# A decoder layer with a routed mixture of experts on one core: the router fed with rows before their norm, work moved between queues at four places, and identity transposes put into TensorE's queue

## The chip, the core and the metric

The kernel runs on one core of one Trainium2 chip. The core has five engines, each with a queue of its own that runs in order: TensorE (PE in the profile; its weight loads are PEld), VectorE (DVE), ScalarE (ACT), GpSimd (POOL) and SyncE (SP), which here only issues DMA transfers. Engines wait for each other by semaphores alone. The metric is the time of one execution on the device, in microseconds (us), as the median of several runs; lower is better.

## The reference, cut to what matters

One inference step of a layer for 1024 prompt rows and 8 sample rows of 1024 numbers, all in float32. It has an attention and short-convolution mixer, an output projection with residual, and then this:

```python
tok = concatenate([_rmsnorm(hp, norm_ffn), _rmsnorm(hs, norm_ffn)])       # 1032 rows
lg = tok @ w_rg + b_rg                                                    # 4 groups
p_group = softmax(lg);  g_sel = argmax(lg)
le = (tok @ w_re + b_re).reshape(T, 4, 8)                                 # 8 experts in each group
top_v, top_i = top_k(le[g_sel], 2)
gates = softmax(top_v) * p_group[g_sel]
# for each expert e, on the rows that chose it:
hid = silu(x @ w_gate[e]) * (x @ w_up[e]);  y = hid @ w_down[e]
out = sum over the two experts of gate * y                                # added to the residual
y_prompt, y_sample = _rmsnorm(h, norm_final)
```

`_rmsnorm(x, g)` is `x * rsqrt(mean(x*x) + eps) * g`. So a row's norm is one number for the row (`rsqrt(...)`) times one number for each column (`g`).

## The kernel before, in words

Every product that must be precise is done with a high and a low half: ScalarE rounds a tile to the high half, VectorE subtracts to get the low half, and TensorE does three matmuls (high by high, low by high, high by low). The stages, in order of time:

1. **Projection (to 329 us).** 24 column tiles of `w_in`, 3 groups of 344 rows each. SyncE loads `w_raw` tiles in turn (`load_win`); `amask`, the attention mask, is loaded when all groups are done (line 523).
2. **Prompt attention (to 457 us).** 32 steps: `scores` (line 753), `mask` on VectorE (line 1425, which reads `amask`), exponent on ScalarE, turned probabilities (line 768), values (line 791). TensorE begins `scores(n+1)` when `mask(n)` has taken both its banks.
3. **Output projection and router (to 610 us).** 9 turns p = 0..8 of up to 128 rows. In a turn TensorE does `project(p, half, c)` (lines 832 to 834), VectorE adds the bank to `xres` (`residual`, line 1498), ScalarE squares and takes the root (`root_ffn`, lines 1165 and 1166), VectorE makes the normed rows `h2` (`router_rows`, lines 1506 and 1507), SyncE stores them in DRAM (`store_h2`, line 567), TensorE turns them (`turn_h2`, line 846), ScalarE copies them to `h2T` (line 1175), TensorE multiplies them with the router's 36 columns (`route`, line 856), and VectorE picks group and two experts (`choose_first`, `choose_second`, lines 1523 to 1550). `rank` (lines 866, 869) counts how many rows before this one took the same expert, `slots_of` (lines 1570 to 1578) makes one-hot slots of it, `place` (line 877) sums them into a table of 32 experts by 96 slots. Most of this runs a turn or two behind the projection. After turn 8, `token_rows` (lines 1606 to 1610) makes row numbers of the table and `gidx` (line 1617) gives them to GpSimd (`routed`).
4. **Experts (to 1205 us).** 32 experts, one block of 96 rows each. GpSimd gathers the rows (`fetch`, line 1811), TensorE turns them (`turn_rows`, line 922), then `gate`, `up` (both lines 932 to 934), `turn_hidden` (line 948) and `down` (lines 961 to 963). SyncE loads 6 MB of weights for each expert into two sets of buffers; ScalarE and VectorE split them (lines 1203 and 1712). There is one high tile for each of gate, up and down (`wd_hi` for down), so ScalarE may write the next one only when TensorE is done with the last. `list_further` (lines 1627 to 1640) counts the experts with more than 96 rows; such an expert would get a further block after the 32. `count_tile(8)` (line 1558) brings the last turn into the sum that the matmul on line 906 spreads.
5. **Tail (to 1257 us).** SyncE loads `gfin` and the experts' rows `y`, VectorE adds them (line 1781) and norms the row (line 1794).

## Time and profile before

| | us |
|---|---|
| median of 3 runs (1256.76 to 1258.24) | 1257.4 |
| the profiled execution | 1259.14 |
| its span in the trace | 1257.3 |
| TensorE busy in the span | 1141.1 (91%) |
| VectorE busy | 845.0 (67%) |
| ScalarE busy | 666.0 (53%) |
| mean granted clock of TensorE | 0.959 |

The granted clock is a share of 2.4 GHz; it has two levels here, 1.00 (2.4 GHz) and 0.50 (1.2 GHz). A row of a timeline gives the start in us from the span's start, the duration in us, the engine, the line of the program, the operation, what it writes `<-` what it reads, the shape and how many of them, and in brackets how long the engine had been idle and who released it. The chain of waits is followed back from the last instruction; its shares say where time would have to be saved. A float32 matmul that is not split stands as two rows in the trace (x16 for the 8 of `route`), a transpose as one.

### The profile page before, as it was taken

The numbers are of one execution on the slowest core, as the hardware profiler recorded it, in microseconds if no ns is written. First come the engines' busy times: TensorE is split into PE (matmuls) and PEld (weight loads), VectorE is DVE, ScalarE is ACT, GpSimd is POOL, SyncE is SP. The second block draws the span as 40 slices with busy tenths as digits, with TensorE's granted clock in tenths as the row PEclk, the third lists the DMA queues.
The fourth block names the chain that finished last, engine by engine and source line by source line (L and its number), as shares of the span: only waits on it lengthen the run. The fifth ranks groups of instructions, "written<-read, shape, count | busy, mean of one in ns | idle before, by whom it ended". The sixth has DMA issues, their size and how long they took to land.

```text
span 1257.3 us, 16967 instructions
## 1 busy us (share of the span) xinstructions
PE 1141.1 (91%) x6776; PEld 905.4 (72%) x6776; DVE 845.0 (67%) x1149; ACT 666.0 (53%) x832; POOL 107.5 (9%) x126
## 2 busy tenths in 40 slices
PE   5899999999899989997399999999999999999820
PEld 4899999999677658886267777777777777777510
DVE  6214434331577747776588888888898888888529
ACT  6212231111267753331367777777777777777513
POOL 0003110021000000000111111111111111111000
PEclk9999999999999999998599999999999999999965
DMA  8115435141211042001879999999999999999346
GB/s 252 36 51 170 137 96 197 48 127 59 85 52 41 1 143 90 40 34 66 328 278 388 391 391 393 397 393 390 388 399 388 393 387 389 398 392 387 110 162 267
DMA packets 76256, 287.18 MB, mean 228 GB/s; under 512 B 8240, under 2 KB 32944, under 8 KB 51600
## 3 DMA queue, kind: packets, MB, share of 16 engines
q1 hardware_dynamic: 64496, 250.33, 52.1%
q0 software_dynamic: 11680, 35.75, 8.7%
q8 instruction: 55, 0.90, 0.3%
q14 instruction: 25, 0.20, 0.0%
HBM read 264.87 MB, written 25.32 MB: 231 GB/s over the span
## 4 chain that ended last, share of the span: by engine, by line
PE 88%; DVE 4%; DMA 3%; ACT 3%; issue 1%; SPq 0%; POOLq 0%; ACTq 0%; DVEq 0%
PE psum L934 10%; PE psum L932 10%; PE psum L933 9%; PE psum L677 8%; PE psum L679 7%; PE psum L678 7%; PE psum L961 5%; PE psum L962 5%; PE psum L963 5%; PE psum L832 3%; PE psum L753 3%; PE psum L768 3%; PE psum L834 3%; PE psum L833 3%; PE psum L791 2%; PE psum L922 2%
## 5 line engine op out<-in xcount | busy, mean ns | idle before, releaser
L677 PE MATMUL psum<-h_hi,w_hi 128*128 128x344 f32 x576 | 187.3, 325 | 4.1 <-DVE h_lo L1362 4.1
L679 PE MATMUL psum<-h_hi,w_lo 128*128 128x344 f32 x576 | 185.5, 322 | 0.0
L678 PE MATMUL psum<-h_lo,w_hi 128*128 128x344 f32 x576 | 185.5, 322 | 0.0
L1712 DVE TENSOR_TENSOR w_down_lo<-w_down,w_down_hi 128x2048 fp32r<-128x2048 f32 x64 | 143.8, 2288 | 54.2 <-ACT w_down_hi L1203 54.2
L1712 DVE TENSOR_TENSOR w_gate_lo<-w_gate,w_gate_hi 128x2048 fp32r<-128x2048 f32 x64 | 143.8, 2288 | 20.2 <-ACT w_gate_hi L1203 20.2
L1712 DVE TENSOR_TENSOR w_up_lo<-w_up,w_up_hi 128x2048 fp32r<-128x2048 f32 x64 | 143.8, 2288 | 3.0 <-ACT w_up_hi L1203 0.2
L1203 ACT CAST w_gate_hi<-w_gate 128x2048 fp32r<-128x2048 f32 x64 | 119.3, 1921 | 0.0
L1203 ACT CAST w_up_hi<-w_up 128x2048 fp32r<-128x2048 f32 x64 | 119.2, 1920 | 0.0
L1203 ACT CAST w_down_hi<-w_down 128x2048 fp32r<-128x2048 f32 x64 | 118.7, 1904 | 0.0
L677 PEld LDWEIGHTS psum<-h_hi,w_hi 128*128 128x128 f32 x576 | 109.6, 190 | 6.2 <-DVE h_lo L1362 4.7
L961 PE MATMUL psum<-w_down_hi,hT_hi 128*96 128x512 f32 x256 | 103.3, 403 | 7.8 <-DVE hT_lo L1732 7.8
L678 PEld LDWEIGHTS psum<-h_lo,w_hi 128*128 128x128 f32 x576 | 109.6, 190 | 0.0
L679 PEld LDWEIGHTS psum<-h_hi,w_lo 128*128 128x128 f32 x576 | 109.6, 190 | 0.0
L1310 DVE TENSOR_TENSOR w_lo<-w_raw,w_hi 128x1024 fp32r<-128x1024 f32 x24 | 29.4, 1224 | 111.8 <-ACT w_hi L1040 111.8
L932 PE MATMUL psum<-w_gate_hi,xT_hi 128*96 128x512 f32 x256 | 101.8, 397 | 3.0 <-issue 1.8
L932 PE MATMUL psum<-w_up_hi,xT_hi 128*96 128x512 f32 x256 | 102.3, 400 | 0.0
L934 PE MATMUL psum<-w_gate_hi,xT_lo 128*96 128x512 f32 x256 | 102.0, 398 | 0.0
L933 PE MATMUL psum<-w_gate_lo,xT_hi 128*96 128x512 f32 x256 | 101.5, 397 | 0.0
L962 PE MATMUL psum<-w_down_lo,hT_hi 128*96 128x512 f32 x256 | 101.4, 396 | 0.0
L963 PE MATMUL psum<-w_down_hi,hT_lo 128*96 128x512 f32 x256 | 101.3, 396 | 0.0
L934 PE MATMUL psum<-w_up_hi,xT_lo 128*96 128x512 f32 x256 | 101.1, 395 | 0.0
L933 PE MATMUL psum<-w_up_lo,xT_hi 128*96 128x512 f32 x256 | 100.7, 393 | 0.0
(226 smaller groups left out, 1946.0 us busy)
## 6 DMA issues: line engine op xcount, KB each, us to landing
w_gate<-in_w_gate SPq DMA_DIRECT2D x64, 1024.0 KB, 10.4
w_up<-in_w_up SPq DMA_DIRECT2D x64, 1024.0 KB, 11.3
w_down<-in_w_down SPq DMA_DIRECT2D x64, 1024.0 KB, 11.0
w_raw<-in_w_in SPq DMA_DIRECT2D x24, 512.0 KB, 3.7
y_tile<-y_rows SPq DMA_DIRECT2D x16, 512.0 KB, 6.5
kv<-in_cache_k POOLq DMA_DIRECT2D x24, 256.0 KB, 3.8
kv<-in_cache_v POOLq DMA_DIRECT2D x24, 256.0 KB, 4.5
x_tile<-in_x_prompt SPq DMA_DIRECT2D x8, 512.0 KB, 5.5
```

The source lines that it names most:

```text
L677: mm(ps[:, 0:TC], wh[:, k, :], h_hi[:, k, cols], start=(k == 0), stop=False)
L678: mm(ps[:, 0:TC], wh[:, k, :], h_lo[:, k, cols], start=False, stop=False)
L679: ins = mm(ps[:, 0:TC], wl[:, k, :], h_hi[:, k, cols], start=False, stop=(k == KD - 1))
L753: ins = mm(bank(2 * h, 2)[:, at:at + w], qT[head, m, i * P:(i + 1) * P], kT[head, m, at:at + w], start=True, stop=True)
L932: mm(bank(b)[0:SLOTS, :], xT_hi[:, k, :], hi[:, k, :], start=(k == 0), stop=False)
L933: mm(bank(b)[0:SLOTS, :], xT_hi[:, k, :], lo[:, k, :], start=False, stop=False)
L934: ins = mm(bank(b)[0:SLOTS, :], xT_lo[:, k, :], hi[:, k, :], start=False, stop=(k == KD - 1))
L961: mm(out, hT_hi[:, m, :], wd_hi[:, m, cols], start=(m == 0), stop=False)
L962: mm(out, hT_hi[:, m, :], wd_lo[s][:, m, cols], start=False, stop=False)
L963: ins = mm(out, hT_lo[:, m, :], wd_hi[:, m, cols], start=False, stop=(m == DE // P - 1))
L1203: nc.scalar.copy(dst[:, part, :], src[:, part, :]).then_inc(ready, 1)
L1712: vec.tensor_tensor(dst[:, part, :], src[:, part, :], hi[:, part, :].bitcast(F32), ALU.subtract).then_inc(split, 1)
```

## The change: what it does

- **Start.** The first tiles of x are loaded in another order among `const`, `gmix` and `w_raw`, and ScalarE does one square root on a cell that GpSimd has cleared before it waits for any input.
- **Mask.** `amask` is loaded during the projection, beside `w_raw` (after the sample scores have been turned), into another place.
- **Router.** The transposes take `xres` in place of `h2`, half a row tile at a time (`turn_half`), so they don't wait for the norm. The column factor of the norm is multiplied into the router's weights once (`wr`, `gffn_k`), and the row factor is applied to the 36 results in `choose_first` (two operations in place of two, and a maximum of its own). `h2` is still made and stored, for the gather.
- **Last turn.** The order on VectorE, ScalarE and TensorE is written out anew for turn 8: choosing for turn 7 stands ahead of the last residual, VectorE copies the second half of the last `h2T`, `route(8)` stands right behind `rank(7)`.
- **Transposes of the identity.** 12 stand ahead of `rank(8)` and 16 behind the wait for `routed`; they write bank 0, and nothing reads them.
- **Loads around the routing.** `w_up` of expert 0 goes ahead of the last `h2` store, and `w_up` and `w_down` of expert 1 wait until the first gather has landed. VectorE begins to split the first gate weights when GpSimd has issued that gather (`fetch_issued`).
- **Last expert.** Its high half of `w_down` gets a tile of its own, in the place of the gate's high tile (`wd_hi_end`); `list_further` is moved there. `gfin` is loaded there too, and the two rows of y have a semaphore each.

The core of the diff:

```diff
@@ load_x, amask, loads (SyncE)
             load_x(0)
             sp.dma_start(cst[:], a["const"]).then_inc(const_in, 16)
+            load_x(1)
             sp.dma_start(gmix, a["norm_mix"].partition_broadcast(P)).then_inc(gmix_in, 16)
+            load_x(2)
             load_win(0)
-            load_x(1)
-            load_x(2)
...
+                if t == MASK_AT:
+                    sp.wait_ge(scored, NS + 1)
+                    sp.wait_ge(sT_ready, 1)
+                    sp.dma_start(amask, a["amask"]).then_inc(mask_in, 16)
...
-            sp.wait_ge(group_done, len(groups))
-            sp.dma_start(amask, a["amask"]).then_inc(mask_in, 16)
...
-            for p in range(NT):
+            for p in range(NT - 1):
                 store_h2(p)
             sp.wait_ge(o_ready, 4 * NT)
             load_up(first, 0, 0)
+            store_h2(NT - 1)
+            load_down(first, 0, 0)
             load_gate(first, 1, 1)
-            load_down(first, 0, 0)
+            sp.wait_ge(first.rows_in, 16)
             load_up(first, 1, 1)
             load_down(first, 1, 1)
...
+            sp.wait_ge(first.up_done, NE)
+            sp.dma_start(gfin, a["norm_final"].partition_broadcast(P)).then_inc(gfin_in, 16)
@@ TensorE
-            def turn_h2(p):
-                w = rows(turn[p])
-                pe.wait_ge(h2_ready, p + 1)
+            def turn_half(p, half):
+                t = turn[p]
+                w = rows(t)
+                pe.wait_ge(o_used, 4 * p + 2 * half + 2)
                 if p >= 1:
                     pe.wait_ge(h2T_copied, 2 * p)
                     pe.wait_ge(lg_used, p)
...
+            pe.wait_ge(o_used, 4 * NT)
+            for k in range(12):
+                nc.tensor.transpose(bank(0)[:, (k % 4) * P:(k % 4 + 1) * P], ident, ident)
             rank(NT - 1)
             place(NT - 1)
-            pe.wait_ge(o_used, 4 * NT)
             pe.wait_ge(summed, NT)
             mm(bank(6)[:, NE:2 * NE], ones, r_sum[NT % 2], start=True, stop=True, skip_group_check=True
                ).then_inc(counted, 1)
...
             pe.wait_ge(routed, 1)
+            for k in range(16):
+                nc.tensor.transpose(bank(0)[:, (k % 4) * P:(k % 4 + 1) * P], ident, ident)
             pe.wait_ge(first.rows_in, 16)
             turn_rows(first)
...
-                    down(first, (b - 1) % 2, b - 1)
+                    down(first, (b - 1) % 2, b - 1, wd_hi_end if b == NE else wd_hi)
@@ ScalarE
+            act.wait_ge(table_warm, 1)
+            nc.scalar.activation(stat[0:1, 83:84], stat[0:1, 82:83], ACT.Sqrt)
...
             def upper_down(n):
-                if n >= 1:
+                if n == NE - 1:
+                    act.wait_ge(first.gate_done, NE)
+                elif n >= 1:
                     act.wait_ge(first.y_done, n)
@@ VectorE
+                vec.scalar_tensor_tensor(out=r_g[0:w, t, :], in0=lg[:, 0:NGRP], scalar=scale, in1=rbias[0:w, 0:NGRP],
+                                         op0=ALU.mult, op1=ALU.add)
+                vec.scalar_tensor_tensor(out=r_le[0:w, :], in0=lg[:, NGRP:NR], scalar=scale, in1=rbias[0:w, NGRP:NR],
+                                         op0=ALU.mult, op1=ALU.add).then_inc(lg_used, 1)
+                step(vec.tensor_reduce(gm, r_g[0:w, t, :], X, ALU.max))
...
+            residual(NT - 1, 1, (0,))
+            choose_first(NT - 2)
+            choose_second(NT - 2)
+            residual(NT - 1, 1, (1,))
+            count_tile(NT - 2)
+            dve.wait_ge(h2T_ready, 2 * NT)
+            vec.tensor_copy(h2T[:, 4:8, :], bank(5).rearrange("p (k t) -> p k t", k=4)).then_inc(h2T_last, 1)
+            recip_ffn(NT - 1)
             slots_of(NT - 2)
+            router_rows(NT - 1)
             choose_first(NT - 1)
             choose_second(NT - 1)
             slots_of(NT - 1)
...
+            dve.wait_ge(fetch_issued, 1)
             lower_gate(first, 0, 0)
-            list_further()
+            count_all()
             lower_rows(first, 0)
...
+                if b == NE - 1:
+                    lower_down(first, b % 2, b, wd_hi_end)
                 if b < NE:
                     hidden(first, b)
...
+                if b == NE - 1:
+                    list_further()
...
-                dve.wait_ge(y_in[t % NY], 32 * (t // NY + 1))
...
                 for c in range(2):
+                    dve.wait_ge(y_in[t % NY][c], 16 * (t // NY) + 16)
@@ GpSimd
             fetch(first, gidx[:, 0:1])
+            gp.memset(stat[0:1, 82:83], 0.0).then_inc(fetch_issued, 1)
```

`count_all` is the first part of what `list_further` was: `count_tile(NT - 1)`, a wait for `counted`, and a copy of the counts.

How instructions stand on TensorE at the end of the router stage, before (after the last `project`; `cst` is the identity or a matrix of ones, `h_0` the normed rows of turn 8, `r_both_152` belongs to turn 7 and `r_both_151` to turn 8):

```order
L866 MATMUL psum<-r_both_152,cst 128x32
L869 MATMUL psum<-r_sum_154,cst 128x32
L877 MATMUL psum<-r_first_148,hot_slot_159 96x32
L877 MATMUL psum<-r_second_150,hot_slot_160 96x32
L846 MATMUL psum<-cst,h_0_120 128x128 x8
L856 MATMUL psum<-wr,h2T 128x36 x8
L866 MATMUL psum<-r_both_151,cst 128x32
L869 MATMUL psum<-r_sum_153,cst 128x32
L877 MATMUL psum<-r_first_147,hot_slot_159 96x32
L877 MATMUL psum<-r_second_149,hot_slot_160 96x32
L906 MATMUL psum<-r_sum_154,cst 128x32
L922 MATMUL psum<-cst,x_rows 128x96 x8
```

And with the change, from the same place to `rank(8)`:

```order
L858 MATMUL psum<-cst,xres 128x128 x4
L882 MATMUL psum<-r_both_152,cst 128x32
L885 MATMUL psum<-r_sum_154,cst 128x32
L872 MATMUL psum<-wr,h2T 128x36 x8
L893 MATMUL psum<-r_first_148,hot_slot_159 96x32
L893 MATMUL psum<-r_second_150,hot_slot_160 96x32
L921 MATMUL psum<-cst 128x128 x12
L882 MATMUL psum<-r_both_151,cst 128x32
```

The second half of the turned rows (L858) and `route(8)` (L872) now stand ahead of `place(7)`, and the 12 transposes behind it.

TensorE between `place(8)` and the first expert, with the change and with the semaphores it waits for:

```order
L925 MATMUL psum<-r_sum_154,cst 128x32 [waits summed]
L987 MATMUL psum<-cst 128x128 [waits routed]
L987 MATMUL psum<-cst 128x128 x15
L941 MATMUL psum<-cst,x_rows 128x96 [waits expert_rows_in]
L941 MATMUL psum<-cst,x_rows 128x96 x7
```

The 16 transposes (L987) stand behind the matmul that spreads the counts (L925, before L906), and ahead of the turning of the gathered rows.

VectorE in the same stretch, with the change, from `gidx` on:

```order
L1663 CAST gidx<-r_tab 96x32
L1665 TENSOR_TENSOR r_134<-r_133,r_132 128x9
L1666 TENSOR_TENSOR r_groups<-r_groups,r_131 128x36
L1761 TENSOR_TENSOR w_gate_lo_189<-w_gate_183,w_gate_hi 128x2048 x2
L1592 TENSOR_TENSOR r_sum_154<-r_sum_153,r_both_151 128x32
L1674 COPY r_count<-psum 128x32
L1752 TENSOR_TENSOR xT_lo<-psum,xT_hi 128x384 x2
L1761 TENSOR_TENSOR w_up_lo_191<-w_up_185,w_up_hi 128x2048 x2
```

`r_sum_154`, for which L925 waits, is still written behind the two halves of the gate weights; the operations of `list_further` that stood between it and `xT_lo` are gone from here.

## Rows read from the trace of the kernel before

**Rows 1.** The page, part 4: share of each engine in the chain of waits.
```profile
PE 88%; DVE 4%; DMA 3%; ACT 3%; issue 1%; SPq 0%; POOLq 0%; ACTq 0%; DVEq 0%
```

**Rows 2.** Stretches: us, each engine's busy time, granted clock, DMA share, GB/s.
```profile
176.30:180.90 4.60, 4.60 (x42) 4.31 (x40) 0.00 (x0) 4.44 (x10) 0.00 (x0) 1.00 0.00 0
487.00:588.00 101.00, 100.33 (x560) 85.79 (x559) 75.86 (x245) 27.45 (x58) 0.00 (x0) 1.00 0.09 36
590.00:592.00 2.00, 0.00 (x0) 0.00 (x0) 1.89 (x5) 0.00 (x0) 0.00 (x0) 0.50 0.00 0
594.40:595.70 1.30, 0.51 (x4) 0.51 (x5) 1.11 (x10) 0.00 (x0) 0.00 (x0) 0.50 1.00 309
622.70:630.90 8.20, 6.82 (x21) 4.79 (x22) 6.38 (x10) 2.24 (x3) 0.93 (x1) 0.50 0.19 49
645.00:1184.00 539.00, 539.00 (x2563) 383.40 (x2562) 471.14 (x305) 414.11 (x334) 68.10 (x59) 1.00 0.99 381
1197.40:1200.90 3.50, 3.50 (x9) 2.30 (x10) 0.00 (x0) 0.00 (x0) 0.00 (x0) 0.50 0.00 0
```

**Rows 3.** Timeline at the end of the projection: start, duration, engine, line, operation.
```profile
329.58 1.99 PE L753 MATMUL psum<-kT,qT 64*128 64x512 f32 x8 [0.81 <-DVE cT L1376]
332.13 1.23 DVE L1425 CUSTOM_DVE_ANT_0 scores<-psum,amask 128x1024 f32<-128x1024 f32 x1 [2.80 <-DMA amask<-in_amask]
334.56 3.38 PE L753 MATMUL psum<-kT,qT 64*128 64x512 f32 x8 [2.99 <-DVE stat L1425]
```

**Rows 4.** Timeline of the last router turn.
```profile
582.28 1.87 PE L856 MATMUL psum<-wr,h2T 128*128 128x36 f32 x16
587.44 0.75 DVE L1498 SCALAR_TENSOR_TENSOR xres<-psum,stat,xres 128x512 f32<-128x512 f32 x1 [4.21 <-PE psum L834]
590.60 1.29 DVE L1507 SCALAR_TENSOR_TENSOR h<-xres,stat,gffn 128x1024 f32<-128x1024 f32 x1
595.85 1.95 PE L846 MATMUL psum<-cst,h 128*128 128x128 f32 x8
598.47 3.63 PE L856 MATMUL psum<-wr,h2T 128*128 128x36 f32 x16 [0.68 <-ACT h2T L1175]
602.14 0.19 DVE L1523 TENSOR_TENSOR rl<-psum,rbias 128x32 f32<-128x32 f32 x1 [6.55 <-PE psum L856]
605.52 0.19 DVE L1550 TENSOR_TENSOR r_both<-r_first,r_second 128x32 f32<-128x32 f32 x1
```

**Rows 5.** Timeline from the row numbers to the first expert.
```profile
609.65 0.17 DVE L1617 CAST gidx<-r_tab 96x32 int32<-96x32 f32 x1
609.92 4.48 DVE L1712 TENSOR_TENSOR w_gate_lo<-w_gate,w_gate_hi 128x2048 fp32r<-128x2048 f32 x2
610.71 4.55 POOL L1811 DMA_INDIRECT x_rows<-h_rows,gidx  x1 [316.93 <-DVE gidx L1617]
614.65 0.61 PE L906 MATMUL psum<-r_sum,cst 128*128 128x32 f32 x2 [6.10 <-DVE r_sum L1558]
622.88 1.51 PE L922 MATMUL psum<-cst,x_rows 96*128 96x96 f32 x8 [7.62 <-DMA x_rows<-h_rows,gidx]
625.60 0.71 PE L932 MATMUL psum<-w_gate_hi,xT_hi 128*96 128x512 f32 x1 [1.21 <-ACT xT_hi L1193]
```

**Rows 6.** All gathers of the run: duration ns min/median/max, first and last start.
```profile
L1811 POOL DMA_INDIRECT x_rows<-h_rows,gidx x32: 932/1306/4552, 610.7 to 1149.3; - x32
```

**Rows 7.** The chain of waits at the end, in order of time: start, us, what.
```profile
1190.25 1.91 ACT w_down_hi L1203
1192.17 4.49 DVE w_down_lo L1712 x2
1204.88 1.02 ACT y_rows L1218
1206.67 4.28 DMA y_rows<-y_rows,sidx
1212.95 6.06 DMA y_tile<-y_rows
```

More of the change, by code:

```diff
@@ L259, in program @@
         ot = [pack(f"out_tile{s}", [D]) for s in range(NO)]
-        gfin = pack("gfin", [D])
         fjunk = pack("fjunk", [D])
@@ L383, in program @@
         first = Flow("expert")
-        y_in = [sem(f"y_in{s}") for s in range(NY)]
+        y_in = [[sem(f"y_in{s}_{c}") for c in range(2)] for s in range(NY)]
         gfin_in = sem("gfin_in")
@@ L1172, in copy_h2T @@
                     act.wait_ge(lg_ready, p)
-                for half in range(2):
+                for half in range(halves):
                     act.wait_ge(h2T_ready, 2 * p + half + 1)
@@ L1495, in residual @@
                 x = xres[0:w, t, half * 512:(half + 1) * 512]
-                for c in range(2):
+                for c in branches:
                     dve.wait_ge(o_ready, 4 * p + 2 * half + c + 1)
@@ L1500, in residual, with recip_ffn @@
                     dve.wait_ge(o_used, 4 * p + 2 * half + c + 1)
+            def recip_ffn(p):
+                c, w = p % 2, rows(turn[p])
+                dve.wait_ge(std_f_ready, p + 1)
+                step(vec.reciprocal(rst_f[0:w, c:c + 1], std_f[0:w, c:c + 1]))
             def router_rows(p):
```

130 lines of the change are left out of this document (73 added, 57 removed).

## The prediction

> **What bounds the kernel now.** I read the chain of waits first. TensorE holds 88% of it [rows 1], so the question is where TensorE stands still or runs at half clock. The table of stretches answers that. In the router turns it is busy for 100.3 of 101 us at full clock, and in the experts from 645 to 1184 for all of 539 us [rows 2]. In both the change puts no more work on TensorE and takes none away, and there is no idle time to win. Between these stages lie the holes. The timelines and the end of the chain show four: the wait for the mask at 329 us [rows 3], the last router turn [rows 4], the way from the row numbers to the first expert [rows 5], and the last expert with the tail [rows 7]. The change touches all four. I take its parts in that order, each as time by which everything behind it starts earlier.
>
> **Start.** The tile of x that the chain passes through is the fourth, which has the same bytes ahead of it as before. The early square root saves ScalarE a table load where it waits for data anyway. 0, with 0.5 lost and 1.4 won as ends (1.4 is one transfer of 512 KB at the 381 GB/s of [rows 2]).
>
> **Mask.** Before, VectorE began the first mask at 332.13, released by the load of `amask`. With the mask there it waits for the scores. TensorE began them at 329.58 and was done 1.99 later [rows 3], and VectorE can start some 0.1 to 0.2 behind that, at 331.7. So 0.4 won. The second scores took 3.38 where the first took 1.99, since the clock had halved in 2.99 us of idleness. That idleness shrinks to 2.6. From 587.4 (the last projection ends) TensorE is idle, and at 590.0 it stands at 0.50 [rows 2]: 2.6 us were enough there. So I leave this loss in place; if the clock held, 1.4 more. The load itself moves beside the loads of `w_raw`. A wait is added on SyncE, and queued behind it are the `w_raw` tiles, each loaded two column tiles (some 23 us) ahead of its use; the wait ends with the column tile that is running when it begins. Nothing follows.
>
> **Turns 0 to 7.** The same 8 transposes and the same `route` stand in the queue of TensorE, one wait behind another. The new maximum in `choose_first` is one more small step of VectorE (0.2), which has 25 us to spare in this stretch [rows 2]. The one multiplication of `wr` lies ahead of turn 0, beside the wait for `xres`. 0, between 0.7 won (all that TensorE is idle for) and 0.5 lost.
>
> **Last turn, the largest term.** Before, the last residual ran from 587.44 to 588.19. Then VectorE finished turn 7 and TensorE turned the rows only at 595.85, multiplied them until 602.10 at half clock, and the choice for turn 8 began at 602.14 [rows 4].
> With the change, step by step:
> - `route(7)` ends at 584.15 (582.28 + 1.87). `turn_half(8, 0)` waits until VectorE has taken its logits (0.4) and takes 0.5 (4 transposes; 8 took 1.95 at half clock, so 1.0 at full). The last projection moves back by 0.9 and the last residual ends at 589.1.
> - The second half is turned by 589.7 and copied by VectorE by 590.5 (0.75, as its other pass over 128x512 out of PSUM). Then `route(8)`: 1.87 at full clock gives 592.4; at half clock 3.63 gives 594.1.
> - VectorE meanwhile has the reciprocal (0.2), the slots of turn 7 (1.3, 594.4 to 595.7 [rows 2]) and the normed rows (1.29): it is free at 593.3. TensorE has had no gap above 1 us, so I take 592.4, and VectorE is the later one.
> - The choice took 602.14 to 605.71, 3.6 us, and now 3.8. So turn 8 is chosen at 597.1. The 12 transposes end before that: behind `place(7)` at 592.9, 12 x 0.24 at most gives 595.8. They hide behind VectorE's choice, and cost nothing until the choice ends before them.
> - From there to `gidx` it was 4.1 us (605.71 to 609.82 [rows 4, 5]), and the path is the same.
> So `routed` stands at 601.2 where it stood at 609.8: 8.6 won. With `route` at half clock 7.8; with all of it at full clock 9.2. The store of `h2` for turn 8 goes behind the 2 MB of `w_up` and has from 593.3 to 600 for 0.5 MB; it is hidden by some 3 us.
>
> **From `routed` to the first expert.** Before: 13.1 us from `gidx` to the turning of the rows (622.88), 2.7 more to the first `gate` matmul (625.60). The gather's issue took 4.55 us beside VectorE's split of the gate weights, and 0.93 where it was shortest [rows 5, 6]. Now VectorE waits for it, so the rows land earlier. The scatter that left GpSimd with the DMA engines free landed 4.28 after its start [rows 7]; the first gather landed 7.6 after the end of its issue, with 10 MB of weights under way. So the rows land 5.2 to 9.5 us behind `routed`. But look at the orders of TensorE and VectorE. The 16 transposes stand behind the matmul L925, which waits for `r_sum_154`, and VectorE writes that behind the split. The split now starts at `routed` + 2.0 (0.9 to the issue, 0.9 for it, 0.2 for the semaphore) and ends at + 6.5. L925 starts 0.25 later and takes 0.6: + 7.3. Only then come the 16 transposes, at half clock, since TensorE has stood for 5 us: 16 x 0.244 = 3.9. So the gathered rows are turned from + 11.2, whenever they landed: not in the shadow of the gather but behind it. 13.1 - 11.2 = 1.9 won. Without the transposes it would be up to 3.9 more.
>
> **The clock of the first expert.** Before, it ran at 0.50 for 8.2 us up to 630.9, of which 5.3 were `gate` matmuls [rows 2, 5]. If the transposes bring the clock up, the 5.3 us shrink by half and the turning from 1.51 to 0.8: 2.6 + 0.6 = 3.2 won. Do transposes count as work for the clock? From 176.3 to 180.9 TensorE did transposes alone (41 of 42 rows) and kept 1.00 for 4.6 us, where 2.6 us of nothing lost it [rows 2]. That is keeping and not raising, but I take it for yes: 3.2, between 0 and 3.2.
> The Trainium skill speaks against it. "TensorE: Matmul & The Clock Gate", Part 4, PE-mode transpose, says that full clock "doesn't engage" for transposes, which don't count as busy in the same way. By that rule this term is 0; the stretch at 176.3 speaks against it for keeping, and no row here decides it for raising.
>
> **Experts 0 to 30.** The order is the same. What is new is that `w_up` and `w_down` of expert 1 are issued with the rows' landing. They are 4.2 MB, some 11 us at 381 GB/s, and the second `up` comes some 20 us after the first `gate`. 0, with 2 lost as the other end.
>
> **Last expert.** Before, ScalarE began the high half of the last `w_down` at 1190.25, after the copy of y; VectorE ended the low half at 1196.7, and TensorE went on at 1197.4 [rows 2, 7]. Now ScalarE and VectorE do both while TensorE is in `up` and `down` of the two last experts. What is left behind the copy of y are the two halves of the turned hidden rows. The low half with the start of `down` took 0.7 before (1196.66 to 1197.40), and I give the high half 0.5: 1191.5. 5.9 won. `list_further` now stands ahead of that low half on VectorE. I estimate 4 us for its ten passes, each between the 0.19 of a small one [rows 4] and the 1.23 of a wide one [rows 3]. Counted from the end of the last `gate`: 1 us of small work on ScalarE, 3.8 for its two high halves (1.91 each), 2.8 until VectorE has the second low half, 0.7 for `hid`, 4 for the list: 12.3. The low half of the hidden rows is wanted at 13: `up` and `down` (5.5 each), the turning (0.5) and ScalarE's 1.5. So it is just covered by `down(30)`; each us over is lost. TensorE is idle for 1.9 us there and not 7.8, so the 3.5 us at half clock [rows 2] become 1.8: 1.7 more. Sum 7.6, between 5 and 7.8.
>
> **Tail.** `y` no longer has 512 KB of `gfin` ahead of it, and VectorE starts when the first of two rows is there. The first tile landed 6.06 after its issue at 1212.95 [rows 7]. Three transfers of 512 KB lay in that, and one goes: 1.6. The other 1.3 is the first addition, which now runs beside the second transfer. Behind that VectorE is without a gap. 2.9, between 2.0 and 3.2.
>
> **The sum.** 0 + 0.4 + 0 + 8.6 + 1.9 + 3.2 + 0 + 7.6 + 2.9 = 24.6. The profiled execution took 1259.1 and would take 1234.5. The median of the runs shown, 1257.4, lies 1.7 below that execution, so I forecast 1232.8. A measurement of this kernel can tell about 0.2%, 2.5 us, from no change.
>
> **Rivals.**
> - The transposes of the identity don't raise the clock: the first expert starts at half clock and the 3.9 us are paid for nothing. For it: in this trace only stretches of real matmuls raised the clock. Against it: the stretch at 176.3. 24.6 - 3.2 = 21.4: 1236.0. Chance 0.2. This is also what the page's rule gives.
> - The idleness at the mask is now short enough to keep the clock: 1.4 more, perhaps with a little at the start: 1231.0. For it: 2.6 us is at the edge of what lost the clock elsewhere. Chance 0.12.
> - The last expert gets less than half of its gain, since its `w_down` is issued only at y's release two experts ahead, or `list_further` pushes out the low half of the hidden rows. For it: VectorE's load there has 0.7 us of slack by my steps. Against it: loads land in about 11 us. 4 to 5 less: 1237.5. Chance 0.1.
> - The change doesn't do what it says: the first gather still waits for the stream of weights, and its rows land behind + 11.2. For it: 4.2 MB are issued just ahead of it. Against it: they need 11 us from 593.3, and end at 605. It would cost up to 3: 1236. Chance 0.06.
> - Slower: the rows are now rounded in another order ahead of the router, and one choice of an expert falls the other way, so that one expert passes 96 rows. Today there are exactly 32 gathers [rows 6]. A further block runs with nothing beside it: 6 MB of weights (16 us), their split (4), the three products (17.5) and gather and scatter (8), about 45 us: 1278. It decides with the 97th row of any expert. Against it: only ties in the last digits can flip. Chance 0.03.
> My forecast keeps 0.49.
>
> **The numbers.** The likeliest case alone lies between 1230.5 and 1235.5 by the ends of its terms. The range must take in the first four cases and their mixtures: 1227.5 to 1239.5. All but the last are faster by far more than 2.5 us. Faster 0.95, within 0.2% 0.02 (several terms failing at once), slower 0.03.
>
> **What would show it.** In the profile after: the first mask released by the scores near 331.7; `route(8)` right behind the last residual; `gidx` near 601; the 16 transposes starting about 7.3 us behind it, with a gather that landed before; the granted clock at the first `gate`; TensorE's gap ahead of the last `down` near 2 us, at full clock; the first addition of y 5 us behind its issue. I am wrong in the main point if `gidx` is later than 603, if the experts' stretch is longer than before for the same 30 experts, or if the rows are turned before the split of the first gate weights has ended.

## The result

| | before | after |
|---|---|---|
| time, median of 4 runs | 1257.3 us (1256.8 to 1258.2) | 1239.5 us (1236.8 to 1241.3) |
| ratio | | 0.9856, 95% interval 0.9835 to 0.9876 |
| profiled execution, span | 1259.1, 1257.3 us | 1238.5, 1236.7 us |
| TensorE in the chain of waits | 88% | 85% |

The forecast was 1232.8 us, with a range of 1227.5 to 1239.5. The median lies at the range's very edge: 17.8 us were won of the 24.6 forecast. A second set of seven runs had a median of 1236.5 and went from 1234.1 to 1246.8. That spread of 12.7 us, where nine runs of the kernel before beside them spread over 3.1, is part of what has to be explained.

The same milestones in both profiled executions, and what lies between them. All but the end are starts of an instruction, in us; the turns are counted from their square sums, the first matmuls of a turn:

| from, to | before | after | won | forecast |
|---|---|---|---|---|
| start, first square sum of turn 0 | 457.16 | 454.28 | 2.9 | 0.4 |
| turns 0 to 7 | 115.1 | 120.0 | **-4.9** | 0 |
| turn 8, to `gidx` | 37.4 | 27.9 | 9.5 | 8.6 |
| `gidx`, rows turned | 13.2 | 10.7 | 2.5 | 1.9 |
| first turning, second turning | 16.3 | 15.1 | 1.2 | 3.2 |
| to the copy of y, expert 30 | 550.1 | 550.1 | 0 | 0 |
| to the copy of y, expert 31 | 15.5 | 9.7 | 5.9 | 7.6 |
| to the end | 52.4 | 48.9 | 3.5 | 2.9 |

The sum is 20.6, the difference of the two spans.

### The profile page after: what moved, and what is told of

It reads as the page before. It is cut to its first block, busy times and chain, and to the rows that moved or that the text cites. A ratio compares the mean times of both kernels' runs of the same rounds, so it can differ in the third digit from the quotient of the medians.

```text
span 1236.7 us, 17046 instructions
## 1 busy us (share of the span) xinstructions
PE 1142.0 (92%) x6804; PEld 906.7 (73%) x6804; DVE 848.4 (69%) x1151; ACT 664.9 (54%) x831; POOL 104.2 (8%) x128
## 4 chain that ended last, share of the span: by engine, by line
PE 85%; DVE 7%; issue 3%; ACT 3%; DMA 1%; SPq 0%; POOL 0%; POOLq 0%; DVEq 0%; ACTq 0%
PE psum L953 10%; PE psum L951 10%; PE psum L952 10%; PE psum L689 8%; PE psum L691 7%; PE psum L690 7%; PE psum L980 5%; PE psum L982 5%; PE psum L981 5%; PE psum L765 3%; PE psum L780 3%; PE psum L803 2%; PE psum L844 2%; PE psum L941 2%; PE psum L846 2%
## 5 line engine op out<-in xcount | busy, mean ns | idle before, releaser
L1761 DVE TENSOR_TENSOR w_down_lo<-w_down,w_down_hi 128x2048 fp32r<-128x2048 f32 x62 | 139.3, 2289 | 46.5 <-ACT w_down_hi L1226 46.5
L1226 ACT CAST w_down_hi<-w_down 128x2048 fp32r<-128x2048 f32 x62 | 115.1, 1905 | 0.0
L980 PE MATMUL psum<-w_down_hi,hT_hi 128*96 128x512 f32 x248 | 99.3, 401 | 0.0
L982 PE MATMUL psum<-w_down_hi,hT_lo 128*96 128x512 f32 x248 | 97.6, 394 | 0.0
```

Source lines behind the costliest of these rows:

```text
L980: mm(out, hT_hi[:, m, :], wd_hi[:, m, cols], start=(m == 0), stop=False)
L982: ins = mm(out, hT_lo[:, m, :], wd_hi[:, m, cols], start=False, stop=(m == DE // P - 1))
L1226: nc.scalar.copy(dst[:, part, :], src[:, part, :]).then_inc(ready, 1)
L1761: vec.tensor_tensor(dst[:, part, :], src[:, part, :], hi[:, part, :].bitcast(F32), ALU.subtract).then_inc(split, 1)
```

## The profile after

The chain, answering to [rows 1]:
```profile
PE 85%; DVE 7%; issue 3%; ACT 3%; DMA 1%; SPq 0%; POOL 0%; POOLq 0%; DVEq 0%; ACTq 0%
```
Stretches (us, busy time of PE, PEld, DVE, ACT, POOL, granted clock, DMA share, GB/s), answering to [rows 2]:
```profile
470.00:571.00 101.00, 99.49 (x556) 84.39 (x555) 79.42 (x236) 30.52 (x66) 0.00 (x0) 1.00 0.10 41
568.00:570.00 2.00, 1.70 (x16) 1.58 (x16) 1.93 (x12) 0.00 (x0) 0.00 (x0) 1.00 0.00 0
571.00:574.00 3.00, 3.00 (x8) 2.33 (x8) 0.00 (x0) 0.00 (x0) 0.00 (x0) 0.50 0.00 0
595.30:597.00 1.70, 1.70 (x10) 1.70 (x10) 1.46 (x9) 1.70 (x2) 0.00 (x0) 0.50 1.01 419
599.00:601.00 2.00, 1.11 (x8) 1.00 (x8) 1.11 (x10) 1.98 (x2) 0.00 (x0) 1.00 0.99 397
609.10:614.40 5.30, 5.30 (x26) 5.01 (x26) 0.20 (x2) 0.48 (x1) 0.00 (x0) 0.50 0.38 97
634.00:1173.00 539.00, 539.00 (x2562) 383.42 (x2561) 474.31 (x306) 417.69 (x336) 68.14 (x59) 1.00 0.99 381
1178.40:1180.40 2.00, 0.01 (x2) 0.03 (x1) 0.60 (x2) 1.15 (x2) 0.44 (x1) 1.00 0.00 0
1181.50:1184.50 3.00, 3.00 (x9) 1.98 (x8) 0.00 (x0) 0.00 (x0) 0.00 (x0) 0.51 0.27 75
```
The experts' stretch is the same to the hundredth. In the router turns TensorE, idle for 0.7 of 101 us before, is idle for 1.5. And two stretches that were at full clock before are at half clock: 571 to 574, behind a wait of 0.3 us, and the start of turn 0 (to 458), behind waits of 0.2 to 0.9 us that the kernel before has as well.

The mask, answering to [rows 3]:
```profile
328.52 1.99 PE L765 MATMUL psum<-kT,qT 64*128 64x512 f32 x8 [0.81 <-DVE cT L1404]
330.63 1.23 DVE L1453 CUSTOM_DVE_ANT_0 scores<-psum,amask 128x1024 f32<-128x1024 f32 x1 [2.37 <-PE psum L765]
333.06 1.99 PE L765 MATMUL psum<-kT,qT 64*128 64x512 f32 x8 [2.55 <-DVE stat L1453]
```
VectorE waits for the scores and no longer for the load. The second scores run at full clock here (1.99 for 3.38).

The last turn, answering to [rows 4], in order of time:
```profile
590.34 0.75 DVE L1526 SCALAR_TENSOR_TENSOR xres<-psum,stat,xres 128x512 f32<-128x512 f32 x1
592.75 2.04 PE L872 MATMUL psum<-wr,h2T 128*128 128x36 f32 x16 [0.57 <-DVE h2T L1642]
595.23 2.79 PE L921 MATMUL psum<-cst 128*128 128x128 f32 x12
598.77 0.19 DVE L1584 TENSOR_TENSOR r_both<-r_first,r_second 128x32 f32<-128x32 f32 x1
602.22 0.17 DVE L1663 CAST gidx<-r_tab 96x32 int32<-96x32 f32 x1
```
`route(8)` follows the last residual, at full clock but for its last 0.3 us; the choice is done 6.75 us earlier than in [rows 4]. From there to `gidx` it takes 3.45 instead of 4.13 us: the clock had come up again at 597.9, while the last of the 12 transposes ran.

From the row numbers to the first expert, answering to [rows 5]:
```profile
603.27 0.98 POOL L1864 DMA_INDIRECT x_rows<-h_rows,gidx  x1 [310.56 <-DVE gidx L1663]
604.38 4.49 DVE L1761 TENSOR_TENSOR w_gate_lo<-w_gate,w_gate_hi 128x2048 fp32r<-128x2048 f32 x2 [1.81 <-POOL stat L1900]
609.03 0.63 PE L925 MATMUL psum<-r_sum,cst 128*128 128x32 f32 x2 [7.91 <-DVE r_sum L1592]
609.48 3.65 PE L987 MATMUL psum<-cst 128*128 128x128 f32 x16
612.11 0.80 SPq L563 DMA_DIRECT2D w_up<-in_w_up  x2
612.92 1.49 PE L941 MATMUL psum<-cst,x_rows 96*128 96x96 f32 x8
615.62 0.71 PE L951 MATMUL psum<-w_gate_hi,xT_hi 128*96 128x512 f32 x1 [1.21 <-ACT xT_hi L1216]
```
SyncE's issue at 612.11 waits for the gathered rows: they had landed by then, 0.8 us ahead of their turning. The gather's issue took 0.98 us beside a VectorE that waits, where it had taken 4.55.

All gathers, answering to [rows 6]:
```profile
L1864 POOL DMA_INDIRECT x_rows<-h_rows,gidx x32: 947/1306/2581, 603.3 to 1138.1; - x32
```
Still exactly 32, so no expert got a further block.

The end of the chain, answering to [rows 7]:
```profile
1178.16 1.01 ACT y_rows L1241
1179.58 0.57 DVE hT_lo L1781
1180.40 0.44 PE psum L980
1187.83 1.02 ACT y_rows L1241
1189.62 3.99 DMA y_rows<-y_rows,sidx
1194.77 3.62 DMA y_tile<-y_rows
1198.50 1.29 DVE xres L1834
```

## Why the router turns became longer

The waits of TensorE in the turns name it. Columns: who waited for what, us in total, times, longest. After:
```profile
PE psum L893 <- DVE hot_slot L1609: 1.5, 5, 0.3
PE psum L858 <- DVE rl L1557: 0.3, 1, 0.3
```
The second is the wait of `turn_half(8, 0)` for VectorE, for which the prediction had 0.4. The first is new: the kernel before has no wait above 0.15 us in these turns. `place` (L893) multiplies the one-hot slots, and VectorE writes them too late. Follow VectorE through one turn, in the kernel before:
```profile
527.11 0.75 DVE L1498 SCALAR_TENSOR_TENSOR xres<-psum,stat,xres 128x512 f32<-128x512 f32 x1 [2.48 <-PE psum L834]
538.33 0.57 DVE L1575 TENSOR_SCALAR hot_slot<-cst,r_rank_of 128x96 f32<-128x96 f32 x2
538.71 0.35 PE L877 MATMUL psum<-r_first,hot_slot 128*96 128x32 f32 x2
```
and after:
```profile
526.56 0.75 DVE L1526 SCALAR_TENSOR_TENSOR xres<-psum,stat,xres 128x512 f32<-128x512 f32 x1 [2.48 <-PE psum L846]
538.10 0.57 DVE L1609 TENSOR_SCALAR hot_slot<-cst,r_rank_of 128x96 f32<-128x96 f32 x2
538.49 0.35 PE L893 MATMUL psum<-r_first,hot_slot 128*96 128x32 f32 x2 [0.31 <-DVE hot_slot L1609]
```
VectorE stands still for 2.48 us in each turn, but all of it lies at one place, ahead of the last residual: 20.3 of the 25 us that it is idle in [rows 2] lie there, and the rest are starts of less than 0.1 us between its small steps. Behind that place it works without a wait through the choice, the normed rows, the next turn's split and first residual up to the slots: 11.22 us before, 11.54 after. The new maximum and the two scaled steps are the 0.32. Before, the first of the two slots was done at 538.66 and `place` came at 538.71, 0.05 us behind it. That is the distance at which `place` starts in the changed kernel too, where it waits for the slot, and it is the same in each of turns 3 to 7 of the kernel before. So there was no slack at all: this path already set the pace before the change, with waits too short to show. The 0.32 us went through whole, to a turn of 15.48 for 15.14.

The bigger loss is the clock. In turn 7 it fell behind the 0.3 us wait between narrow matmuls (row 568 to 570), and project(7, 1, 1) ran at 0.63 for a matmul of 0.40: that turn took 17.05. So the 4.9 us lost in turns 0 to 7 are three things, rounded: 1.8 by the longer path in turns 2 to 7, 1.6 by the clock in turn 7, and 1.6 by the clock at the start of turn 0, where no slot is involved yet.

## The experiments

All are the changed kernel with the edit shown, where nothing else is said. Ratios are against the kernel before on the same chip. A length of a turn is the distance of two square sums in the profile.

**The changed kernel again (after_again).**

> The changed kernel once more, unaltered, as the ruler for the other three of this call. Its first four runs spread over 4.5 us where the kernel before spread over 1.5. Theory A: the missing time is a fixed wait of 0.3 us in each of five router turns, the same in each run, and stretches at half clock (turn 0 and turn 7, 1.6 and 1.9 us) that come or stay away by run. Then this profile shows the five waits again (1.5 us in all on hot_slot), and the half-clock stretches in other turns or none; time 1236 to 1242. Rival B: the half-clock stretches belong to fixed places of the program; then turns 0 and 7 are again 12.7 and 17.0 us long.

1236.5 us (1234.1 to 1246.8, 7 runs), 0.982 (0.9806 to 0.9833). The profiled run was the slowest, 1246.8. Its turns: 12.61, 13.04, 15.34, and then five times 17.04.
```profile
PE psum L893 <- DVE hot_slot L1609: 1.6, 5, 0.4
509.00:512.00 3.00, 2.69 (x14) 2.22 (x14) 1.69 (x11) 0.00 (x0) 0.00 (x0) 0.80 0.00 0
```
The waits are the same (theory A), but the half-clock stretch now stands behind the wait of each turn from 3 on. The wait is fixed, the fall of the clock behind it comes or stays away by run: 1.6 us for each turn that has it, up to 8 in one run. That is most of the spread. Turn 0 was at half clock again. The second scores at the mask took 3.50 us at half clock this time: what looked like 1.4 us won there in the first profile is not the change's.

**The waiting matmuls behind the last projection (place_late).**
```diff
-                if p >= 2:
+                if p == NT:
                     place(p - 2)
...
                 if p < NT:
                     project(p, 1, 1)
+                if 2 <= p < NT:
+                    place(p - 2)
```


> The two placing matmuls of a turn stand behind the last projection of that turn instead of ahead of it, for turns 2 to 8. Theory A (TensorE stands for hot_slot, since VectorE's chain from the residual over the choice to the slots ends 0.3 us too late): the five waits go, turns 3 to 7 are 15.14 us long as before, 1.5 us less than the unaltered changed kernel. If the 0.3 us gap in a stretch of narrow matmuls is also what lets the clock fall in turn 7, 1.9 more in the runs that have it: 3.4. Rival B (VectorE is the bound of the turn's loop, and the wait only moves to the next thing that TensorE needs from it, the square sums or the residual): 0, turns stay at 15.48.

1234.4 us (1232.4 to 1237.1, 5 runs), 0.9815 (0.9801 to 0.9829). TensorE waits nowhere from 465 to 575, and `place` comes 3 us behind its slots:
```profile
470.00:568.00 98.00, 98.00 (x554) 83.33 (x553) 78.15 (x235) 29.32 (x63) 0.00 (x0) 1.00 0.11 46
535.40 0.57 DVE L1611 TENSOR_SCALAR hot_slot<-cst,r_rank_of 128x96 f32<-128x96 f32 x2
538.48 0.28 PE L893 MATMUL psum<-r_first,hot_slot 128*96 128x32 f32 x2
```
The turns from 3 on took 14.9 us, shorter than the 15.14 of before, which neither theory had; it fits a kernel before in which `place` was already waiting. The same held in each of the six later profiles with this edit, and none of the seven has a half-clock stretch in turns 1 to 7, while each of the five with the wait has one to five. Against the unaltered kernel run beside it (after_again) the medians differ by 2.1 us, but the intervals overlap; the turns in the profiles carry the verdict: theory A.

**The same loss made in the kernel before (before_steps).** Two idle steps in `choose_first`:
```diff
+                step(vec.tensor_copy(r_e4[0:w, :], r_ng[0:w, t, :]))
+                step(vec.tensor_copy(r_pen[0:w, :], r_e4[0:w, :]))
```


> The kernel before, with two idle copies of 128x4 (0.2 us each) added to choose_first on VectorE; nothing else is touched. Theory A (VectorE's chain from the last residual of a turn to the slots is the loop that paces the turns; in the kernel before it had 0.1 us of slack, and the new choice is 0.3 us longer): TensorE begins to wait for hot_slot in the turns from 2 on, some 0.3 us each, and the clock halves in some turns as it did in the changed kernel; turns 15.5 to 17.0 us instead of 15.14, the whole 2 to 10 us slower plus 0.4 in the last turn. Rival B (VectorE has 25 us to spare and the lengthening of the turns in the changed kernel comes from TensorE's own new order): no waits, turns as before, 0.4 slower at most.

1269.2 us, 1.0097 (1.0081 to 1.0112): 0.4 us of work in each turn, for an engine that is busy for 76 of 101 us [rows 2], costs 11.7 us.
```profile
PE psum L877 <- DVE hot_slot L1577: 2.1, 5, 0.4
495.00:581.00 86.00, 83.94 (x424) 70.97 (x423) 61.38 (x200) 23.71 (x50) 0.00 (x0) 0.90 0.08 32
```
The turns took 15.4 and then five times 17.15. Rival B falls: nothing of the changed kernel's order is in this one. The expectation's "0.1 us of slack" was too much, as shown above.

**The later place in the kernel before (before_place_late).** The edit of place_late, in the kernel before.

> The kernel before with one edit, the placing matmuls of turns 2 to 7 behind the last projection. Theory A (VectorE's loop gave TensorE 0.1 us of slack, and the order of TensorE alone costs 0.24 us in a turn, since in place_late the turns took 14.9 us where the kernel before has 15.14): turns 14.9, 1.2 to 1.5 us faster, 1256. Rival B (the 14.9 comes from the turning of the raw rows in two halves, new in the changed kernel): turns stay 15.14, no difference.

1256.0 us (11 runs), 0.9992 (0.9983 to 1.0001). The turns took 14.97, so 0.17 of the 0.24 is TensorE's order alone (theory A), which fits the wait hidden in the kernel before; in the time, the interval just takes in no difference.

**Without the transposes of the identity (no_idents).**
```diff
-            for k in range(12):
-                nc.tensor.transpose(bank(0)[:, (k % 4) * P:(k % 4 + 1) * P], ident, ident)
...
-            for k in range(16):
-                nc.tensor.transpose(bank(0)[:, (k % 4) * P:(k % 4 + 1) * P], ident, ident)
```


> The changed kernel without both sets of transposes of the identity (the 12 and the 16). Theory A (they neither raise nor keep the clock where it matters, and the 16 only stand in the way of the gathered rows, which landed at about 612.0 while they were turned from 612.9): the rows are turned 0.9 us earlier, the half-clock stretch of the first gate is 0.9 to 1.5 longer, so 0 to 0.6 slower or no difference; the ranking of turn 8 runs at half clock, 0.3 lost. Rival B (they do raise the clock, only late): without them gate(0) stands 5.3 us at half clock as in the kernel before, where it is 2.6 with them: 1.3 to 1.7 slower in sum. Rival C (they are pure cost): 0.9 faster.

1241.2 us (4 runs), 0.9854 (0.9835 to 0.9872). Slower than the 1236.5 of the unaltered one, but three of its turns were at half clock (17.05), ahead of anything that the edit touches, and the unaltered kernel's own runs went up to 1246.8. So the times decide nothing here, and the pieces of the profile have to. `gidx` to the turned rows: 9.8 instead of 10.7 us. From the choice to `gidx`: 4.15 instead of 3.45, at half clock:
```profile
602.00:606.00 4.00, 1.88 (x8) 1.64 (x8) 2.08 (x17) 3.18 (x2) 0.00 (x0) 0.50 1.01 412
622.00:628.00 6.00, 6.00 (x28) 4.17 (x27) 2.01 (x7) 2.02 (x2) 0.00 (x0) 1.00 1.01 354
```
The clock came up 2.8 us into gate(0) (at 621.6), no later than with the 16 transposes (2.6 and 2.8). So the 16 cost 0.9 us and gave nothing that a profile shows (theory C for them). What they cost hangs on the landing of the rows: in the four profiles that have them at this place, the rows had landed 8.7 to 9.9 us behind `gidx`, and were turned at 10.7 in all four. The 12 gave 0.7 in this comparison of two profiles. A kernel without any of these transposes, before_steps, also had its clock up 2.8 us into gate(0), and the same 15.2 us from the first turning to the second as the changed kernel.

**8 real matmuls in place of the 16 (wide8).**
```diff
-            for k in range(16):
-                nc.tensor.transpose(bank(0)[:, (k % 4) * P:(k % 4 + 1) * P], ident, ident)
+            pe.wait_ge(first.gate_hi, 2)
+            for k in range(8):
+                mm(bank(0), wg_hi[:, k % KD, 0:P], wg_hi[:, k % KD, :], start=True, stop=True)
```


> The 16 transposes of the identity are replaced by 8 matmuls of real data, 128x512, into the same spare bank, at the same place; 0.46 us each at half clock, so 3.7 us as before. Theory A (transposes do not count as work for the clock, real matmuls do): the clock is up when gate(0) starts or within 1 us of it, where it took 2.6 us; 1.3 us less, and up to 0.7 more if the rows are already turned at full clock. Rival B (it is only a matter of how long TensorE has been kept busy, whatever with): the same as the unaltered changed kernel, clock up 2.6 us into gate(0).

1241.6 us (1236.1 to 1247.3, 5 runs), 0.9854 (0.9829 to 0.988). The clock came up 2.8 us into gate(0), in after_again 2.8 us as well: rival B. As there, five turns of this profile were at half clock, which the time shows. Here the kind of work makes no difference.

**The mask's load at its old place (pl_mask_late)**, on top of place_late.
```diff
-                if t == MASK_AT:
...
+            sp.wait_ge(group_done, len(groups))
+            sp.dma_start(amask, a["amask"]).then_inc(mask_in, 16)
```

> The changed kernel with the placing matmuls behind the last projection (1234.4 in the last call), and the load of the mask back at its old place, behind the end of the projection. Theory A (the load alone made the hole at the mask: 0.4 of waiting, and 1.4 since the clock fell in the 3 us of idleness and stays in the 2.55): first mask 2.5 us behind the first scores instead of 2.1, second scores 3.4 us at half clock instead of 2.0, 1.8 slower. Rival B (the clock falls or stays there by chance of the run, as the unaltered changed kernel showed 3.5 us once in its second profile): 0.4 slower and the rest as it comes.

1233.9 us, 0.9812 (0.9799 to 0.9825): no difference to place_late (0.9815). The first mask came 2.52 us behind the first scores instead of 2.11, the 0.4 of the forecast, and the second scores ran at full clock though TensorE had been idle for 3.0 us. Rival B; the 0.4 itself is too small for the times.

**The counting matmul and the 16 beside the gather (pl_early_count)**, on top of place_late.
```diff
+            count_tile(NT - 1)
             dve.wait_ge(fetch_issued, 1)
...
-                count_tile(NT - 1)
                 dve.wait_ge(counted, 1)
```

> As place_late, with the sum of turn 8 taken on VectorE ahead of its wait for the fetch, so that the counting matmul and the 16 transposes run at once behind the row numbers, beside the gather. Theory A (the 16 stand 0.9 us in the way of rows that have landed): the rows are turned 9.7 us behind gidx instead of 10.7, 0.9 to 1.0 faster; the clock of the first gate stays at half for 2.6 us or, since TensorE now stands still in between, up to 5.3 as in the kernel before: 0 to 1.3 back. Rival B (the gather's landing sets the turning): no change in the turning.

1232.4 us, 0.9794 (0.978 to 0.9807). The rows were turned 9.8 us behind `gidx` instead of 10.7: theory A, 0.9 won in the profile; in the times the two intervals overlap. The clock came up 3.7 us into gate(0).

**24 real matmuls there instead (pl_early_wide)**, on top of that.
```diff
-            for k in range(16):
-                nc.tensor.transpose(bank(0)[:, (k % 4) * P:(k % 4 + 1) * P], ident, ident)
+            pe.wait_ge(first.gate_hi, 2)
+            for k in range(24):
+                mm(bank(0), wg_hi[:, k % KD, 0:P], wg_hi[:, k % KD, :], start=True, stop=True)
```

> As pl_early_count, but with 24 matmuls of 128x512 (the weights' high half, into the spare bank) in place of the 16 transposes: TensorE is busy from the row numbers to about the landing of the rows. Theory A (the clock comes up behind some 3 to 6 us of unbroken work, whatever the work, and the 16 transposes come too late and are too few): the clock is up before the rows are turned; the turning takes 0.8 instead of 1.5, gate(0) runs at full clock from its start: 1.3 and 0.7, with the 0.9 of the earlier rows 2 to 3 faster than place_late. Rival B (the clock falls again in the 1.2 us between the turning and gate(0)): only the 0.9 and 0.7.

1232.2 us (1231.8 to 1232.7), 0.9798 (0.9785 to 0.9811).
```profile
599.20:604.00 4.80, 4.80 (x12) 3.76 (x13) 3.55 (x2) 0.00 (x0) 1.07 (x2) 0.50 1.02 410
604.00:607.00 3.00, 3.00 (x14) 2.47 (x13) 1.04 (x2) 0.00 (x0) 0.00 (x0) 0.96 0.32 92
609.30:620.50 11.20, 11.13 (x48) 7.81 (x49) 8.16 (x10) 4.72 (x4) 0.00 (x0) 1.00 1.02 390
```
The clock came up in the fill, some 5 us into it, and stayed: the first expert ran at full clock from its start, and from `gidx` to the second turning it took 22.3 us instead of 25.4. (0.9 of this is that the rows landed and were turned earlier in this profile.) But the median is no better than that of pl_early_count. In the profiles, most of the 3.1 us won here went back: at half clock in the last `down`, which pl_early_count's profiled run did not have (1.5), and in 0.9 us more from the copy of y to the end.

**The gain of the last norm ahead of y again (gfin_last)**, on top of pl_early_wide.
```diff
-            sp.wait_ge(first.up_done, NE)
-            sp.dma_start(gfin, a["norm_final"].partition_broadcast(P)).then_inc(gfin_in, 16)
...
             sp.wait_ge(all_sent, 1)
+            sp.dma_start(gfin, a["norm_final"].partition_broadcast(P)).then_inc(gfin_in, 16)
```

> As pl_early_wide, with the load of the last norm's gain back at its old place, ahead of the loads of y. Theory A (512 KB stood ahead of y): the first addition begins some 1.3 to 1.6 us later behind the copy of y, and the whole is 1.6 slower, 1233.8 against 1232.2. Rival B (the end is set by the stream of all y tiles and not by its first, and the DMA engines are idle between): less than 0.5.

1233.3 us, 0.9812 (0.9798 to 0.9825). The first addition began 13.2 us behind the copy of y instead of 10.9, but from the copy of y to the end it was only 0.9 more: with `gfin` early, VectorE starts sooner and then waits 1.7 us for the next tile of y; with it late it runs without a wait. Between A and B. The 0.9 is the least that it can be read as: in the ten other profiles with the early `gfin`, the way from the copy of y to the end took 48.6 to 50.5 us, and here 51.4.

**The last expert without the wait for a copy (best_a).** pl_early_wide with 22 matmuls in place of 24, and:
```diff
+                if b == NE:
+                    act.wait_ge(first.sent, 16 * (b - 2))
+                    copy_y(first, b - 2)
...
+                        down(first, (b - 1) % 2, b - 1, wd_hi_end, 4)
```


> pl_early_wide with 22 instead of 24 filling matmuls, and for the last expert: its hidden rows' high half is cast ahead of the copy of y for expert 30, and down(31) writes two other banks, so that it does not wait for that copy. Theory A (the copy of y, 1.0 us, is all that holds the last down back): TensorE's gap ahead of down(31) is 1.1 instead of 2.0 us, 0.9 faster; 0.2 to 0.5 more from the two matmuls that stood behind the landed rows. The clock in down(31) falls or stays up by run as before. Sum 1.1 to 1.4: 1231. Rival B (the scatter of expert 30 then ends later and holds the copy of y for expert 31): 0.

1229.6 us (1228.4 to 1229.6), 0.978 (0.9766 to 0.9793): 2.6 faster than pl_early_wide by the medians, though the intervals of the ratios overlap. TensorE's gap ahead of `down(31)` was 0.8 shorter (1.2 for 2.0) and the clock stayed up there. Turn 0 was at full clock in this profile and at half in that of pl_early_wide (1.7), which is not the edit's. It fell in gate(0) in this profile, where the 22 matmuls had ended 0.7 us ahead of the turning.

**And four matmuls in the gap left (best_b).**
```diff
+                        for k in range(4):
+                            mm(bank(0), wu_hi[:, k % KD, 0:P], wu_hi[:, k % KD, :], start=True, stop=True)
```

> As best_a, with 4 matmuls of 128x512 on spent data in the gap ahead of down(31). Theory A (the gap of 1 to 2 us is what lets the clock fall at the start of down(31), 1.7 us in the runs that have it; five of the seven profiles so far): the clock stays at 1.00 through down(31), 0 to 1.7 faster than best_a, 1230. Rival B (the narrow transposes and the gap behind them are not the reason, or the gap is too short to matter once it is 1.1): the same as best_a.

1228.6 us (1227.7 to 1229.3), 0.9773 (0.976 to 0.9787): 28.7 us faster than the kernel before, 8 to 11 faster than the changed one.
```profile
1170.00 0.48 ACT L1244 CAST hT_hi<-psum 128x384 fp32r<-128x384 f32 x1 [6.79 <-PE psum L969]
1170.51 0.56 DVE L1791 TENSOR_TENSOR hT_lo<-psum,hT_hi 128x384 fp32r<-128x384 f32 x1 [0.60 <-ACT hT_hi L1244]
1171.17 0.45 PE L982 MATMUL psum<-w_down_hi_end,hT_hi 128*96 128x512 f32 x1 [0.25 <-issue]
1172.40:1176.90 4.50, 4.47 (x20) 2.88 (x18) 0.00 (x0) 0.00 (x0) 0.69 (x1) 1.00 0.20 56
```
`down(31)` starts 0.1 us behind the low half of its rows and runs at full clock. Whether the four matmuls did that stays open: best_a's profile had it without them, and the intervals overlap. (The count in the expectation was off: the clock had fallen in seven of the eight profiles with the gap of 2.0.)

## Why the prediction was right in its direction and short by 7 us

- **Turns 0 to 7, the step that failed.** "One more small step of VectorE (0.2), which has 25 us to spare in this stretch": the busy time was read right and means nothing here. Of the 25 us, 20.3 lie ahead of one instruction of each turn; the path from there to `hot_slot` had no slack. The step was also mis-sized, 0.32 us and not 0.2. The ends I gave (0.7 won, 0.5 lost) were far too near: measured were 4.9 lost in one profile and 11.1 in the other, of which 1.5 and 1.6 are waiting. before_steps and place_late show it from both sides. To name who waits for what is queued behind the added step would have found `place`. Not all of the loss is this step's: 1.6 and 1.5 us are the clock in turn 0, which stays open (below).
- **Start and mask.** The first mask came as computed: 2.1 us behind the scores' start, 0.4 won. The projection ended 1.06 earlier; in before_steps and before_place_late, which don't have the new order of loads, it ended 1.35 and 1.98 earlier, so this comes by run too. The rival "short idleness keeps the clock" came true in the first profile and not in the second, and pl_mask_late kept it with more idleness: not the change's doing. So of the 2.9 us won here, 2.5 are not shown to be the change's.
- **Last turn.** 8.6 forecast, 9.5 measured, by the steps named. The residual ended at 591.09 and not 589.1, since the turns before had lost their time. I had left out that the 12 transposes can bring the clock up for `rank` and `place`: 0.7. In six later profiles the clock was at half there in spite of them (4.13 us), so even that comes by run: four of the ten profiles with the 12 have it.
- **From `gidx` to the rows.** The order was read right: the 16 transposes ran behind L925 and began 7.1 us behind the end of `gidx` (7.3 forecast), and the rows stood landed for 0.8 us. 2.5 us were won for 1.9 forecast. The transposes cost 0.9 and not "up to 3.9", as the rows themselves landed only 9.7 us behind the end of `gidx`, where the prediction had 5.2 to 9.5.
- **Clock of the first expert.** 3.2 forecast, 1.2 measured. From 609.1 to 614.4 TensorE turned matrices without a gap and stayed at half; it came up 2.6 us into gate(0), in no_idents 2.8, and in before_steps, whose kernel has neither the transposes nor the rest of the change, 2.8 as well. It took 5.3 and 5.2 in the two other profiles without the change. So the 1.2 is not shown to be the change's either. The rival (no gain, chance 0.2) was the truth for the 16, but not for its reason. The Trainium skill, "TensorE: Matmul & The Clock Gate", Part 4, PE-mode transpose, says that full clock "doesn't engage" for transposes. Four of these traces don't agree: the clock fell at 594.5, from 595.23 on TensorE did nothing but 12 transposes, and by their end it stood at 1.00 (rows 595.30 and 599.00 above). In the other six profiles with the 12 it stayed at half behind them. And 8 real matmuls in the place of the 16 did no better than they. The 22 or 24 real ones had run for 4.1 to 5.8 us when the clock came up, and the 16 with the turning for 5.3 when it had not: that transposes are worth less is not shown here.
- **Last expert.** The 5.9 for the moved work came (5.87). The 1.7 for the clock did not: TensorE kept its full clock through the 2.0 us gap, and lost it 1 us into `down(31)`, for as long as before. That happened in eight of the nine profiles with this gap. `list_further` was covered, as computed: its last step ended 1178.44, 1.1 us ahead of the low half of the hidden rows.
- **Tail.** 2.9 forecast, 3.5 measured; 1.9 to 3.8 over the later profiles. The first addition came 3.6 us earlier behind the copy of y (10.7 for 14.2), and 3.7 us behind the issue of y, where the prediction had 5.

In sum: 4.9 lost in the turns and 3.7 short in the two clock terms, against 4.6 more than forecast elsewhere, gives the 4.0 between 24.6 and 20.6. Of the 4.6, 2.5 are those of the start that are not shown to be the change's. That the median stayed within the range is in part luck: one more turn at half clock would have taken it out. The other 2.8 lie between profile and medians: the profiled execution of before stood 1.8 above its median, the one of after 1.0 below.

What stays open: why turn 0 was at half clock in eight of the fourteen profiles of all kernels (12.4 to 12.8 us) and not in the others (11.1). The waits of TensorE ahead of it are the same in before and after. But all eight are among the eleven profiles with the change, and none among the three without it, so that the change has a part in it is not excluded.

## What to carry to other kernels

Slack is a property of a path, not of an engine's share. Before a step is added to an engine that "has time", find its idle time's place in the loop and follow the chain from there to the next instruction that another engine waits for; in a software pipeline that path can be full while the engine is 25% idle. An instruction that starts just behind its releaser, turn after turn, is probably waiting already, even where no wait is listed. Where the consumer can be queued later at no cost (here two small matmuls behind a projection), do that first. And a small wait in a stretch of narrow matmuls costs more than its length when the clock falls behind it: look at the granted clock of several profiles, and at the spread of the runs.

## What the hardware showed that I had not expected

- Behind waits of 0.3 to 0.4 us among the narrow matmuls of a turn, the clock fell to half with TensorE busy throughout (the row from 571 to 574); 1.6 us lost each time. It came in some turns and some runs, with the same instructions.
- TensorE held full clock through idleness of 2.55 us (333.06 in the profile after) and 2.96 us (pl_mask_late), and lost it in 2.55 us at the same place in after_again and in 2.99 [rows 3].
- The indirect DMA's issue took 0.98 us with VectorE waiting, and 4.55 beside VectorE's pass of 128x2048.
